# Eight experts on one core: three big and five small items, a weight ring of 16 units, and a router that ranks by pairs

## The reference, cut to what matters

```python
logits = hf @ w_router + b_router
top_v, top_i = lax.top_k(logits, 2)
top_w = softmax(top_v)
for e in range(8):
    out += combine[:, e:e+1] * ((silu(hf @ w_gate[e]) * (hf @ w_up[e])) @ w_down[e])
h = LayerNorm(ALPHA * h + out)
```

## Time and profile before

| | |
|---|---|
| median of the runs | 1654.53 us |
| profiled execution, its own time | 1653.32 us |
| its span, first to last instruction | 1651.5 us |
| TensorE busy | 1557.0 us (94%) |
| VectorE busy | 963.3 us (58%) |
| ScalarE busy | 738.5 us (45%) |
| DMA queue of the weights | 467.95 MB, 70.9% of 16 engines' span |
| mean granted TensorE clock | 0.973 |

### The profile page before, as it was taken

How to read it: one execution, slowest core, us unless ns; L and a number is a source line. 1 busy time by engine, 2 the same in 40 slices (tenths; PEclk the granted TensorE clock), 3 DMA queues, 4 the chain that set the end, 5 groups by cost and what they waited for, 6 DMA issues and landing times.

```text
span 1651.5 us, 18668 instructions
## 1 busy us (share of the span) xinstructions
PE 1557.0 (94%) x7600; PEld 1140.1 (69%) x7600; DVE 963.3 (58%) x904; ACT 738.5 (45%) x678; POOL 40.2 (2%) x30
## 2 busy tenths in 40 slices
PE   5999888999998999979899999999999999999996
PEld 3977777788886887867788436885368853688633
DVE  5547667455556546666899206993069930599403
ACT  3356654333433446653577105771057720477201
POOL 0000040000000000031000000000000000000000
PEclk9998989999999998989999999999999999999998
DMA  8353254455552452246699999999999999999994
GB/s 306 118 204 115 89 194 163 161 196 178 181 199 104 145 213 103 80 175 252 268 367 374 356 426 425 426 426 397 427 425 426 425 400 426 426 425 426 412 425 190
DMA packets 67013, 473.76 MB, mean 287 GB/s; under 512 B 8064, under 2 KB 8192, under 8 KB 10096
## 3 DMA queue, kind: packets, MB, share of 16 engines
q1 hardware_dynamic: 66096, 467.95, 70.9%
q0 software_dynamic: 832, 4.63, 0.8%
HBM read 471.50 MB, written 1.05 MB: 286 GB/s over the span
## 4 chain that ended last, share of the span: by engine, by line
PE 80%; DVE 9%; DMA 5%; ACT 3%; issue 2%; POOL 1%; SPq 0%; DVEq 0%; ACTq 0%; POOLq 0%
PE ps L1530 20%; PE ps L1531 19%; PE ps L1532 19%; PE ps L1873 11%; DMA raw_a<-in_w_item 4%; PE ps L1907 3%; DVE lo_a L987 2%; PE ps L1847 2%; PE ps L1836 1%; PE ps L1880 1%; ACT w_hi L662 1%; PE ps L1696 1%; PE ps L1560 1%; DMA raw_a<-in_w_mix 1%; DVE small L1003 1%
## 5 line engine op out<-in xcount | busy, mean ns | idle before, releaser
L987 DVE TENSOR_TENSOR lo_a<-raw_a,w_hi 128x2048 fp32r<-128x2048 f32 (+2 forms) x117 | 252.2, 2160 | 199.1 <-ACT w_hi L662 198.1
L662 ACT ACTIVATE w_hi<-raw_a 128x2048 fp32r<-128x2048 f32 (+2 forms) x117 | 209.5, 1796 | 180.0 <-PE ps L1532 174.5
L1530 PE MATMUL ps<-w_hi,act_hi 128*128 128x512 f32 (+1 forms) x640 | 254.8, 398 | 24.3 <-DVE act_lo L1053 11.4
L1531 PE MATMUL ps<-lo_a,act_hi 128*128 128x512 f32 (+1 forms) x640 | 249.8, 390 | 0.0
L1532 PE MATMUL ps<-w_hi,act_lo 128*128 128x512 f32 (+1 forms) x640 | 249.2, 389 | 0.0
L1328 DVE TENSOR_TENSOR lo_a<-raw_a,w_hi 128x2048 fp32r<-128x2048 f32 x81 | 184.3, 2289 | 19.7 <-ACT w_hi L898 18.8
L1530 PE MATMUL ps<-w_hi,x_hi 128*128 128x512 f32 x448 | 177.5, 396 | 9.0 <-DVE lo_a L1328 7.2
L898 ACT ACTIVATE w_hi<-raw_a 128x2048 fp32r<-128x2048 f32 x81 | 155.4, 1918 | 62.5 <-PE ps L1532 58.0
L1328 DVE TENSOR_TENSOR lo_b<-raw_b,w_hi 128x2048 fp32r<-128x2048 f32 x72 | 164.4, 2289 | 21.0 <-ACT w_hi L898 21.0
L1532 PE MATMUL ps<-w_hi,x_lo 128*128 128x512 f32 x448 | 174.6, 390 | 0.0
L898 ACT ACTIVATE w_hi<-raw_b 128x2048 fp32r<-128x2048 f32 x72 | 138.6, 1925 | 52.8 <-PE ps L1532 52.8
(11 more groups left out here) (254 smaller groups left out, 2228.9 us busy)
## 6 DMA issues: line engine op xcount, KB each, us to landing
raw_a<-in_w_item SPq DMA_DIRECT2D x210, 1024.0 KB, 11.4
raw_b<-in_w_item SPq DMA_DIRECT2D x144, 1024.0 KB, 14.7
raw_a<-in_w_mix SPq DMA_DIRECT2D x60, 1024.0 KB, 4.9
raw_w<-in_w_item SPq DMA_DIRECT2D x24, 1024.0 KB, 15.5
raw_a<-in_w_mix SPq DMA_DIRECT2D x8, 512.0 KB, 3.8
ln_gb<-in_ln_mix POOLq DMA_DIRECT2D x2, 1024.0 KB, 5.0
cst<-in_consts SPq DMA_DIRECT2D x1, 1178.0 KB, 20.1
h<-in_x SPq DMA_DIRECT2D x2, 512.0 KB, 8.0
```

Of the source, the lines that this page charges most:

```text
L662: nc.scalar.activation(w_hi[:, HI_SLOT[g], 0:n], raw(slot)[:, 0:n], ACT.Copy).then_inc(s_hi, 1)
L987: nc.vector.tensor_tensor(w_lo(slot)[:, 0:n], raw(slot)[:, 0:n], w_hi[:, HI_SLOT[g], 0:n].bitcast(F32), ALU.subtract).then_inc(s_lo, 1)
L1530: nc.tensor.matmul(dst, xh, wh, start=start, stop=False)
L1531: nc.tensor.matmul(dst, xh, wl, start=False, stop=False)
```

## The change

The sizes. The loop over the last items keeps 14 slots of the ring, so that it stays periodic:

```diff
-SLOTS_A, SLOTS = 7, 14
+SLOTS_A, SLOTS = 7, 16
+LOOP_SLOTS = 14
...
-KIND = "BSBSBSBS"
-POS_RANK = [0, 7, 1, 6, 2, 5, 3, 4]
+KIND = "BSBSSBSS"
+POS_RANK = [0, 7, 1, 6, 5, 2, 4, 3]
...
-OVER, TWICE = 4, 2 * N_EXP
+OVER, TWICE = 5, 2 * N_EXP
...
+    if g >= LOOP_BASE:
+        g = LOOP_BASE - SLOTS + (g - LOOP_BASE) % LOOP_SLOTS
```

In SBUF the constants behind `tri` and the scratch of the mixers (`small_mix`) are given up after the mixers, `x_small` lies over `tri`, and products of the list lie in `prod`, over `d_sb`. One new slot lies over the norm's parameters, so its first load waits until these are used:

```diff
-        shared_at = cursor[0]
+        shared_at = (cst_at + COLS["mfox"][0] * 4 + 31) // 32 * 32
+        small_mix = place("small_mix", [P, SMALL_MIX])
...
+        prod = at("prod", [P, 5 * OVER * TWICE], F32, d_at)
         scat = place("scat", [P, TILES, P])
         gath = place("gath", [P, TILES, P])
-        x_small = place("x_small", [P, KT, 64])
+        x_small = at("x_small", [P, KT, 64], F32, cst_at + COLS["tri"][0] * 4)
...
+                        sp.wait_ge(s_lnd, 2 * DEPTH)
...
-                    hold(sp, s_used, j * ITEM_UNITS + (LOOP_BASE + k - SLOTS + 1))
+                    hold(sp, s_used, j * ITEM_UNITS + (LOOP_BASE + k - LOOP_SLOTS + 1))
```

ScalarE takes ALPHA times `h`, and `add_item` waits for it. VectorE's split of item 0's unit 1 moves out of the mixer:

```diff
             copy_tokens(0, True)
+            nc.scalar.activation(cat[:], h[:], ACT.Copy, scale=ALPHA).then_inc(s_res, 1)
...
                     norm(3, h, ln_gb, (s_gb, 48), adds, router_copy)
-                    split(nb + U_OUT + 5)
...
+                dve.wait_ge(s_res, 1)
```

The router: an expert's rank is the number of experts with a larger logit, or an equal one and a lower number, over all 8 x 8 pairs at once. Its first two are taken. The gap goes to ScalarE. The splits of units 1 and 2 follow behind item 0's gather matrix:

```diff
+            nc.vector.memset(tab, 0.0)
+            nc.vector.tensor_copy(vals[:, 4, :], c("iota8"))
...
-            first_largest(lg, m1, oh1)
-            link(nc.vector.scalar_tensor_tensor(lg2, oh1, -3e38, lg, ALU.mult, ALU.add))
-            first_largest(lg2, m2, oh2)
-            nc.vector.tensor_tensor(sel, oh1, oh2, ALU.add).then_inc(s_sel, 1)
-            nc.vector.tensor_tensor(dd, m2, m1, ALU.subtract).then_inc(s_rd, 1)
-            split(MOE_BASE + 2)
+            link(nc.vector.tensor_tensor(logits, ps[:, 0:TILES, 0:N_EXP], b_rt.unsqueeze(1).to_broadcast(e16), ALU.add))
+            other, own = logits.unsqueeze(2).to_broadcast(e288), logits.unsqueeze(3).to_broadcast(e288)
+            lower = c("lower").rearrange("p (a b) -> p a b", a=N_EXP).unsqueeze(1).to_broadcast(e288)
+            nc.vector.tensor_tensor(pair_gt, other, own, ALU.is_gt)
+            link(nc.vector.tensor_tensor(pair_eq, other, own, ALU.is_equal))
+            link(nc.vector.tensor_tensor(pair_eq, pair_eq, lower, ALU.mult))
+            link(nc.vector.tensor_tensor(pair_gt, pair_gt, pair_eq, ALU.add))
+            link(nc.vector.tensor_reduce(ahead, pair_gt, AX, ALU.add))
+            link(nc.vector.tensor_scalar(sel, ahead, 1.5, None, ALU.is_lt))
+            dve.sem_inc(s_sel, 1)
+            link(nc.vector.tensor_scalar(oh1, ahead, 0.0, None, ALU.is_equal))
+            link(nc.vector.tensor_tensor(oh2, sel, oh1, ALU.subtract))
+            link(nc.vector.tensor_tensor(ahead, oh2, oh1, ALU.subtract))
+            link(nc.vector.tensor_tensor(ahead, ahead, logits, ALU.mult))
+            nc.vector.tensor_reduce(dd.rearrange("p t e -> p (t e)"), ahead, AX, ALU.add).then_inc(s_rd, 1)
             dve.wait_ge(s_rk, 1)
             link(nc.vector.tensor_tensor(rkm, ps[:, 6, 0:TILES * N_EXP].rearrange("p (t e) -> p t e", t=TILES), sel, ALU.mult))
-            link(nc.vector.tensor_scalar(rkm, rkm, -1.0, None, ALU.add))
             gather_matrix(lambda t: rkm[:, t, 0:1], True)
...
-            nc.vector.tensor_scalar(cat[:], h[:], ALPHA, None, ALU.mult)
-            dve.wait_ge(s_re, 1)
...
+            split(MOE_BASE + 1)
             tokens_lo(0, None)
...
+            split(MOE_BASE + 2)
```

The list is built in five pieces with wider instructions, between item 0's splits; `item` calls them behind splits 5, 8, 11, 16 and 19:

```diff
-                splits(3, 6)
+                splits(3, 5)
+                if lists:
+                    lists[0]()
+                splits(6, 6)
                 gate_silu(0)
...
+            def weights():
+                dve.wait_ge(s_re, 1)
+                link(nc.vector.tensor_scalar(w1, ee, 1.0, None, ALU.add))
+                link(nc.vector.reciprocal(w1, w1))
+                link(nc.vector.tensor_tensor(w2, w1, ee, ALU.mult))
+                nc.vector.tensor_tensor(oh1, oh1, wide(w1), ALU.mult)
+                link(nc.vector.tensor_tensor(oh2, oh2, wide(w2), ALU.mult))
+                link(nc.vector.tensor_tensor(cwe, oh1, oh2, ALU.add))
...
+            def positions():
+                link(nc.vector.scalar_tensor_tensor(key, cnt, 8.0, c("tie"), ALU.mult, ALU.add))
+                pair = prod[:, 0:64].rearrange("p (a b) -> p a b", a=N_EXP)
+                link(nc.vector.tensor_tensor(pair, key.unsqueeze(1).to_broadcast(e88), key.unsqueeze(2).to_broadcast(e88), ALU.is_gt))
+                link(nc.vector.tensor_reduce(rank, pair, AX, ALU.add))
+                link(nc.vector.tensor_tensor(at_pos, rank.unsqueeze(1).to_broadcast(e88),
+                                             c("posrank").unsqueeze(2).to_broadcast(e88), ALU.is_equal))
...
+            def by_position():
+                e688 = [P, 6, N_EXP, N_EXP]
+                each = prod[:, 0:6 * N_EXP * N_EXP].rearrange("p (r a b) -> p r a b", r=6, a=N_EXP)
+                link(nc.vector.tensor_tensor(each, at_pos.unsqueeze(1).to_broadcast(e688), vals.unsqueeze(2).to_broadcast(e688), ALU.mult))
+                link(nc.vector.tensor_reduce(tab[:, :, 0:N_EXP], each, AX, ALU.add))
...
+            def overflow():
+                e28 = [P, 2, N_EXP]
+                caps = c("caps").rearrange("p (i e) -> p i e", i=2)
+                nc.vector.tensor_tensor(ov2.rearrange("p (i e) -> p i e", i=2), ov.unsqueeze(1).to_broadcast(e28), caps, ALU.is_gt)
+                halves = over_vals.rearrange("p r (i e) -> p r i e", i=2)
+                nc.vector.tensor_tensor(halves[:, 0:2], item_rk[:, :, 0:N_EXP].unsqueeze(2).to_broadcast([P, 2, 2, N_EXP]),
+                                        caps.unsqueeze(1).to_broadcast([P, 2, 2, N_EXP]), ALU.subtract)
+                link(nc.vector.tensor_copy(halves[:, 2:5], tab[:, 2:5, 0:N_EXP].unsqueeze(2).to_broadcast([P, 3, 2, N_EXP])))
+                link(nc.vector.tensor_tensor_scan(inc, ov2, ov2, 0.0, ALU.add, ALU.max))
+                link(nc.vector.tensor_tensor(exc, inc, ov2, ALU.subtract))
...
+            def overflow_items():
+                o4 = [P, OVER, TWICE]
+                link(nc.vector.tensor_tensor(osel, exc.unsqueeze(1).to_broadcast(o4), c("overj").unsqueeze(2).to_broadcast(o4), ALU.is_equal))
+                link(nc.vector.tensor_tensor(osel, osel, ov2.unsqueeze(1).to_broadcast(o4), ALU.mult))
+                o5 = [P, 5, OVER, TWICE]
+                each = prod[:, 0:5 * OVER * TWICE].rearrange("p (r a b) -> p r a b", r=5, a=OVER)
+                link(nc.vector.tensor_tensor(each, osel.unsqueeze(1).to_broadcast(o5), over_vals.unsqueeze(2).to_broadcast(o5), ALU.mult))
+                nc.vector.tensor_reduce(tab[:, 0:5, N_EXP:POSITIONS], each, AX, ALU.add)
+                link(nc.vector.tensor_scalar(ftab[:, 0:1], inc[:, TWICE - 1:TWICE], 1.0, None, ALU.add))
+                nc.vector.tensor_copy(itab[:, 0:POSITIONS + 1], ftab).then_inc(s_tab, 1)
...
+            item(Item(0), None, 3, (weights, positions, by_position, overflow, overflow_items))
```

TensorE: gather 0 goes to banks 4 and 5, item 0 starts with the first half of its tokens, and fewer transposes keep it busy:

```diff
+        def gather_bank(n):
+            return 4 if isinstance(n, int) and n == 0 else 0
...
-                pe.wait_ge(s_xh, it.n * 2 + 2)
-                if it.big:
-                    pe.wait_ge(s_xl, it.bigs * 2 + 2)
-                project(0, GROUP_GATE[0], 0)
+                def gathered(b):
+                    pe.wait_ge(s_xh, it.n * 2 + b + 1)
+                    if it.big:
+                        pe.wait_ge(s_xl, it.bigs * 2 + b + 1)
+                first = before is None
+                gathered(0 if first else 1)
+                project(0, GROUP_GATE[0], 0, gathered if first else None)
...
-                keep_warm((30, 20)[t])
+                keep_warm((14, 8)[t])
```

More of the change, by code:

```diff
@@ L117, in constants @@
     put("tri", np.concatenate([(p[:, None] + P * k <= s[None, :]) for k in range(TILES)], 1))
-    put("iota", p[None, :])
-    put("iota64", p[None, :] % 64)
+    put("iota", p[None, :] + 1)
+    put("iota64", p[None, :] % 64 + 1)
     put("iota8", np.arange(N_EXP)[None, :])
-    put("first", np.arange(N_EXP)[None, :] - 99.0)
+    put("lower", np.tril(np.ones((N_EXP, N_EXP)), -1).reshape(1, -1))
     put("tie", np.array([1e6] + [7.0 - e for e in range(1, N_EXP)])[None, :])
     put("posrank", np.array(POS_RANK)[None, :])
-    put("cap", np.array([CAP[k] for k in KIND])[None, :])
-    put("cap2", np.array([CAP[k] + CAP["S"] for k in KIND])[None, :])
+    put("caps", np.array([CAP[k] + CAP["S"] * i for i in range(2) for k in KIND])[None, :])
     put("overj", np.arange(OVER)[None, :])
@@ L315, in build, with kept @@
         tri = c("tri").rearrange("p (k s) -> p k s", k=TILES)
-        used = [0]
+        used, used_mix = [0], [0]
         sq = sb_tmp[:, 0:512]
         def scratch(n):
+            a = used_mix[0]
+            used_mix[0] += n
+            return small_mix[:, a:a + n]
+        def kept(n):
             a = used[0]
@@ L349, in build @@
         f_row = scratch(SEQ)[0:NF, :]
```

(37 more changed lines are left out.)

128 lines of the change are left out of this document (49 added, 79 removed).

## The result

The changed kernel takes 1642.74 us in the median of five runs (1642.46 to 1644.20), the one before 1654.35 in the same comparison: ratio 0.9938, 95% interval 0.9920 to 0.9955. It is faster by some 11 us. The forecast was 1633, so the sign is right, the gain about half of what the sum gave, and the time within the range by 0.3 us only, outside the forecast's own 1629 to 1637. The profiled execution has a span of 1642.4 us where the sum had 1630.2: 12.2 us have to be found. It is the longest of the five (the others have 1640.7 to 1641.0), its time 1.5 above the median where the forecast set the median 1.2 above it; so the median misses by 9.7.

A forecast was written before the change was run, and what follows sets the result against it. The bound was to pass from TensorE to the DMA queue: 913.3 (item 0's end) + 693.5 (stream) + 4.6 + 18.8 = 1630.2 us of span, forecast time 1633; own range 1629 to 1637, wider range 1625 to 1643.

The forecast's parts named there:

- The bound passes from TensorE to the transfers: After item 0: with three big and five small items TensorE needs 667.6 us instead of 712.3, so DMA binds.
- The list's pieces: In item 0: five pieces of the item list, about 6.3 us, stall 1.0; item 0 takes 123.3, a gain of 1.3.
- The ring is touched once: At item 2's end the full ring pauses the queue 2 us, with no pause at item 5.
- VectorE's choice: Router, before item 0: the new choice takes 2.1 us in all, 0.6 less than the old 2.7.
- ninth item: Rival: an expert ranked fourth or later exceeds 64 tokens, so 42 more units load, 103.5 us: 1736; chance 0.03.
- Start of item 0: Router to item 0: first product at 790.0, 5.6 us earlier, including 0.8 added for a colder array.
- the rival of stalls: Rival in item 0: colder array (3.5 us) and list pieces (up to 5) put its end near 920: 1640; chance 0.17.
- The stream: Loads after item 0: 57 units landed, 279 left at 2.464 us, 687.5, plus 6.0 of losses: 693.5 us.
- The end: Last item: unit 39 lands 4.9 us before the last; products end 4.6 after the last landing, a gain of 1.9.
- the ring: Rival: the two added slots come late, leaving 281 units and pauses at item 2, 4.9 + 3 more: 1641; chance 0.07.
- pauses with the two units: Stream after item 0: 7.6 us from fewer full-ring pauses and 4.9 from two more units landed.

The follow-up runs named there:

- the repetition: The changed kernel run once more with no edit; median 1643.72 us, span 1641.6, ratio 0.9945 against the kernel before.

## Why the prediction was wrong

**What was right.** The bound passes from TensorE to the transfers: item 4 from 1242 us and item 7 from 1541 us on wait for nearly every unit. The list's pieces cost next to nothing: item 0 took 123.6 us (793.5 to 917.1) for 123.3 forecast, and put first they cost 4.6 more there. The ring is touched once, near 1120, and not at item 5 to any depth. VectorE's choice took 1.9 us, from 782.12 to 784.0, for 2.1. No ninth item came. From the last product to the end it is 18.8 us as before.

**Start of item 0, sized wrong: 3.5 us.** The step was "That makes 789.2; I add 0.8 for a colder array". The array ran at half clock from 772 to past 788 us: 0.9 more at the transposes, 1.6 at the logits, 1.0 at the counts (784.1 to 786.4), and 0.9 by which the eight transposes after them still ran when the gather matrix was ready: 4.4 us where I had 0.8; the choice gave 0.2 back. The Trainium skill, "TensorE: Matmul & The Clock Gate", section "Part 1: The HAM clock gate", says that throttled is the default state and activity releases it, and I had read a longer cold stretch from it. The traces bear that out in part only: the stretch did grow, but with none of these transposes it was no longer than with 14, 8 and 8, and with 30 and 20 one stretch of 4 us came up to 0.89. The bound that I had named (3.5 in the rival of stalls) was nearer, but the text behind it priced 4 us at half speed and the gather, not all that stands in a row there; and the other half of that rival, list pieces that stall item 0, did not come. With the 0.3 us in item 0 the end came at 917.1 for 913.3, 3.8 late.

**The stream, sized wrong: 3.8 us.** The step "what has landed is the unit used plus the ring" counts one unit too many: some 56 were in by bytes, since a load goes out only when a unit is used and the queue had not ended it (2.5 us). The kernel before could have told: its stretches from 920.2 us on add up to some 283 units with the norm's, where the prediction counts 282. The rate over 285 us was 425 for my 425.5 (0.8 us). The rest is 0.5. The queue moved 425 GB/s in every long stretch. The 358 GB/s a core that the Trainium skill, "DMA: Bandwidth & Descriptors", section "Where 436 GB/s comes from", gives for transfers from HBM do not bind this one core: where TensorE waits for loads, the rows show 425. The same passage has a measurement of 425 too.

**The end, sized wrong: 4.7 us.** The step "Bound by loads, unit 39 lands 4.9 before the last" took the landings as evenly spaced up to the moment when the queue's bytes are done. Unit 39 landed 0.2 us before that. Two things are in it. About 1.8 us is there even after the queue was emptied (3.1 for 4.9); a store of 256 KB takes 2.0 us to land, of which 0.6 would be transfer at 426 GB/s, so, if a load is like it, some 1.4 us of a landing is no transfer. The rest, up to 2.9, I put down to the drift, which no row shows directly. In the repetition the whole is 3.0 and not 4.7. In the kernel before TensorE ended 6.5 after the last byte for a reason of its own, and so the rows could not show it.

3.8 + 3.8 + 4.7 = 12.3, by rounding 0.1 over the 12.2 sought. No rival had the late landing at the end. The two nearest in time, 1640 and 1641, each had a part of it: the stalls the cold array, the ring one unit of its two.

**The ledger of terms.** Start 2.1 for 5.6, item 0 1.0 for 1.3, end -2.7 for +1.9, and pauses with the two units 8.7 for 12.5: in all 9.1, which is 1651.5 - 1642.4. Such a sum hides that the parts depend on each other, which the table above shows. With a ring of 14 the stream needs as long as TensorE did, and removing 44.7 us of TensorE's work gives 1.2.

## What to carry to other kernels

When two resources need 210 and 207 us a period, relief for one is worth at most the 3 between them in each period, until the other is relieved as well, and here it was 1.2 us in all; price such a pair of edits together and try each alone. Where transfers bind, take the ready time of the last one from an execution in which they already bind, or add 2 to 5 us to its turn in the queue (4.7 in the changed kernel, 3.0 in its repetition, 2.4 in the kernel with old router and new kinds). Padding on an in-order engine is priced at the low clock and against what stands behind it.
